# Six modulation chunks with buffers of their own, and a new order of the first loads, in a diffusion trunk step

## What is computed

```python
def ada_mods(cond, w, b):
    cond = cond.reshape(-1, D_MODEL)
    mod = (jax.nn.silu(cond) @ w + b)[:, None, :]
    return jnp.split(mod, 6, axis=-1)
...
    for i in range(DEPTH):
        sh1, sc1, g1, sh2, sc2, g2 = ada_mods(cond, ada_w[i], ada_b[i])
        h = modulate(rmsnorm(x, norm_mix[i]), sh1, sc1)
        ...
        x = x + g1 * mix
        h = modulate(rmsnorm(x, norm_ffn[i]), sh2, sc2)
        x = x + g2 * conv_ffn(h, ffn_w_in[i], ffn_conv_w[i], ffn_conv_b[i], ffn_w_out[i])
```

## Time and profile before

| | us |
|---|---|
| median of 3 runs | 2990.75 |
| lowest, highest | 2989.33, 2991.61 |
| profiled execution, first to last instruction (span) | 2988.2 |
| PE busy (share) | 2801.6 (94%) |
| DVE busy | 1607.8 (54%) |
| ACT busy | 1184.5 (40%) |
| POOL busy | 109.7 (4%) |

### The profile page before, as it was taken

How to read it: one execution, slowest core, us unless ns; L and a number is a source line. 1 busy time by engine, 2 the same in 40 slices (tenths; PEclk the granted TensorE clock), 3 DMA queues, 4 the chain that set the end, 5 groups by cost and what they waited for, 6 DMA issues and landing times.

```text
span 2988.2 us, 51513 instructions
## 1 busy us (share of the span) xinstructions
PE 2801.6 (94%) x19936; PEld 2645.5 (89%) x19936; DVE 1607.8 (54%) x2878; ACT 1184.5 (40%) x2042; POOL 109.7 (4%) x71
## 2 busy tenths in 40 slices
PE   5977799999998999999989999999998779999999
PEld 4965699999998999999969999999997569999999
DVE  2667556625644664366342665366367754663662
ACT  2347445414423552243232543244234754541441
POOL 1000010000002000000201000000100001000000
PEclk7989899999999999999989999999998989999999
DMA  6410133323320332333201332333121002221222
GB/s 233 181 64 1 50 125 134 137 74 135 136 93 33 138 134 103 123 133 130 66 24 57 120 134 100 111 134 127 63 78 36 1 15 61 78 84 64 73 85 74
DMA packets 62431, 279.67 MB, mean 94 GB/s; under 512 B 7392, under 2 KB 9568, under 8 KB 49632
## 3 DMA queue, kind: packets, MB, share of 16 engines
q1 hardware_dynamic: 62304, 277.93, 27.0%
HBM read 274.74 MB, written 3.16 MB: 93 GB/s over the span
## 4 chain that ended last, share of the span: by engine, by line
PE 86%; DVE 6%; ACT 6%; issue 2%; DMA 1%; SPq 0%; POOL 0%; DVEq 0%; ACTq 0%
PE ps L457 73%; ACT prob L923 3%; PE ps L541 3%; PE ps L480 3%; PE ps L743 1%; PE ps L552 1%; DVE prob L1265 1%; DVE prob L1282 1%; PE ps L502 1%; DMA ada_w<-in_ada_w 1%; ACT stat L925 1%; PE ps L680 1%; PE ps L649 1%; PE ps L510 1%; PE ps L635 1%
## 5 line engine op out<-in xcount | busy, mean ns | idle before, releaser
L457 PE MATMUL ps<-h_hi,w_hi 128*128 128x322 f32 x3392 | 799.8, 317 | 7.2 <-DVE w_lo L1057 4.1
L457 PE MATMUL ps<-h_lo,w_hi 128*128 128x322 f32 x3392 | 784.8, 313 | 0.0
L457 PE MATMUL ps<-h_hi,w_lo 128*128 128x322 f32 x3392 | 780.6, 312 | 0.0
L803 ACT ACTIVATE w_hi<-w_raw 128x1024 fp32r<-128x1024 f32 (+1 forms) x288 | 325.5, 1130 | 1037.1 <-PE ps L457 921.1
L457 PEld LDWEIGHTS ps<-h_hi,w_hi 128*128 128x128 f32 x3392 | 569.6, 190 | 34.0 <-issue 28.4
L457 PEld LDWEIGHTS ps<-h_lo,w_hi 128*128 128x128 f32 x3392 | 577.4, 190 | 0.0
L457 PEld LDWEIGHTS ps<-h_hi,w_lo 128*128 128x128 f32 x3392 | 577.0, 190 | 0.0
L1057 DVE TENSOR_TENSOR w_lo<-w_raw,w_hi 128x1024 fp32r<-128x1024 f32 (+1 forms) x288 | 377.3, 1310 | 67.6 <-ACT w_hi L803 65.9
L1177 DVE SCALAR_TENSOR_TENSOR x<-ps,mods,x 128x321 f32<-128x321 f32 (+5 forms) x264 | 99.9, 435 | 537.1 <-PE ps L457 537.1
L457 PE MATMUL ps<-f_hi,w_hi 128*128 128x322 f32 x1408 | 325.1, 312 | 0.0
L457 PE MATMUL ps<-f_hi,w_lo 128*128 128x322 f32 x1408 | 324.5, 312 | 0.0
(11 more groups left out here) (119 smaller groups left out, 2533.1 us busy)
## 6 DMA issues: line engine op xcount, KB each, us to landing
ada_w<-in_ada_w SPq DMA_DIRECT2D x96, 1024.0 KB, 5.5
w_raw<-in_w_in SPq DMA_DIRECT2D x176, 512.0 KB, 3.6
w_raw<-in_w_out SPq DMA_DIRECT2D x64, 704.0 KB, 4.0
w_raw<-in_w_qkv SPq DMA_DIRECT2D x24, 512.0 KB, 5.1
w_raw<-in_w_o SPq DMA_DIRECT2D x16, 512.0 KB, 3.8
w_raw<-in_w_fnet SPq DMA_DIRECT2D x8, 512.0 KB, 3.6
x<-in_x SPq DMA_DIRECT2D x1, 2576.0 KB, 15.5
out_y<-x SPq DMA_DIRECT2D x8, 322.0 KB, 3.7
```

Of the source, the lines that this page charges most:

```text
L457: mm = pe.matmul(ps[:, 2 * par + hf, 0:NH], w[par][:, kk, :], b[:, hf * NH:(hf + 1) * NH], start=(kk == 0 and n == 0), stop=(kk == k - 1 a ...
L803: act.activation(w_hi[par][:, 0:k, :], w_raw[par][:, 0:k, :], ACT.Copy).then_inc(hi_made, 1)
```

## The change

Chunks 2 to 7 get buffers of their own, `first_w`, that lie over the idle space of the ffn and the mixers, and semaphores of their own, so none of their loads waits. SP gives out nine constants, then chunks 0 and 1, `x`, chunks 2 to 7, the weights of units 0 and 1, and `conv` last. `conv` has its own semaphore, on which ACT and DVE wait ahead of the ffn of layer 0. Because the attention's tables go where `first_w` is, SP waits until all eight chunks are multiplied before it loads them. `chunk_turn` gives the count of earlier loads into an `ada_w` buffer, which is three less from chunk 8 on. What ACT, DVE, POOL and PE do, and in which order, is otherwise the same.

```diff
@@ buffers and semaphores
             tab_raw = sb("tab_raw", [P, 10, 512], F32, a)
+        with ExitStack() as a:
+            first_w = [sb(f"first_w{c}", [P, KT, AW], F32, a) for c in range(2, FIRST_CHUNKS)]
         stage_store = sb("stage_store", [P, 64 * 256 + 64])
...
+        first_in = [sem(f"first_in{c}") for c in range(2, FIRST_CHUNKS)]
+        conv_in = sem("conv_in")
...
-                  (pick, "pick"), (two_heads, "two_heads"), (ident, "ident"), (conv, "conv"),
+                  (pick, "pick"), (two_heads, "two_heads"), (ident, "ident"),
@@ SP
             for dst, src in CONSTS:
                 sp.dma_start(dst[:], t[src]).then_inc(const_in, 16)
-            load_units(0, 2)
             for c in range(2):
                 load_chunk(c, c, chunk_rows(c))
             sp.dma_start(x[:], t["x"]).then_inc(x_in, 16)
             for c in range(2, FIRST_CHUNKS):
-                load_chunk(c, c % 2, chunk_rows(c))
+                sp.dma_start(first_w[c - 2][:], chunk_rows(c)).then_inc(first_in[c - 2], 16)
+            load_units(0, 2)
+            sp.dma_start(conv[:], t["conv"]).then_inc(conv_in, 16)
+            sp.wait_ge(ada_mm, FIRST_CHUNKS)
@@ PE
+            def chunk_turn(c):
+
+                return c // 2 if c < 2 else c // 2 - (FIRST_CHUNKS - 2) // 2
+
             def ada_multiply(c, par, turn):
 
-                pe.wait_ge(ada_in[par], turn * 16 + 16)
+                if isinstance(c, int) and 2 <= c < FIRST_CHUNKS:
+                    weights = first_w[c - 2]
+                    pe.wait_ge(first_in[c - 2], 16)
+                else:
+                    weights = ada_w[par]
+                    pe.wait_ge(ada_in[par], turn * 16 + 16)
...
-                                       ada_w[par][:, 4 * r + j, :], start=(r == 0), stop=(r == 1),
+                                       weights[:, 4 * r + j, :], start=(r == 0), stop=(r == 1),
...
             for c in range(FIRST_CHUNKS):
-                ada_multiply(c, c % 2, c // 2)
+                ada_multiply(c, c % 2, chunk_turn(c))
@@ ACT, ahead of the ffn
+                if layer == 0:
+                    act.wait_ge(conv_in, 16)
@@ DVE, ahead of the ffn
+                if layer == 0:
+                    dve.wait_ge(conv_in, 16)
```

More of the change, by code:

```diff
@@ L664, in _ @@
                         if layer == 0 and FIRST_CHUNKS + n < NCH:
-                            ada_multiply(FIRST_CHUNKS + n, n % 2, (FIRST_CHUNKS + n) // 2)
+                            ada_multiply(FIRST_CHUNKS + n, n % 2, chunk_turn(FIRST_CHUNKS + n))
                         if layer == 0 and 12 < n <= NCH - FIRST_CHUNKS:
@@ L768, in _ @@
                     if not last:
-                        ada_multiply(c0, 0, c0 // 2)
+                        ada_multiply(c0, 0, chunk_turn(c0))
                     with pe.Fori(0, HALF // 2) as i:
@@ L778, in _ @@
                                 else:
-                                    ada_multiply(i * 2 + (c + 1), (c + 1) % 2, i + (c + 1) // 2)
+                                    ada_multiply(i * 2 + (c + 1), (c + 1) % 2, i + chunk_turn(c + 1))
                     if not last:
                         ada_turn(c0 + HALF - 1)
-                        ada_multiply(c0 + HALF, (c0 + HALF) % 2, (c0 + HALF) // 2)
+                        ada_multiply(c0 + HALF, (c0 + HALF) % 2, chunk_turn(c0 + HALF))
                     def gated(kk):
```

## The result

The changed kernel takes 3006.08 us (median of 4 runs, 3005.53 to 3007.95) against 2990.04 for the kernel before on the same chip (4 runs, 2988.77 to 2991.61). The ratio is 1.0057, 95% interval 1.0042 to 1.0071: 16.0 us slower. The forecast was 3006.4, the range 2999 to 3010.

What follows compares the result with a forecast made beforehand. PE carries 86% of the span, but the start hangs on the chain of waits up to copy 7. Copy 7 moving from 48.10 to 63.8 adds 15.7: 2990.75 + 15.7 = 3006.4 us, range 2999 to 3010.

Steps and rivals of the forecast that it cites:

- Where the loss is made: Start of the kernel: weights land at 36.5, w_lo ends at 38.8, copy 0 at 38.85, copy 7 at 63.8.
- The sum: First chunks' chain: copy 7 moves from 48.10 to 63.8, 15.7 us later, added to the median of 2990.75.
- The order on DVE as the cause: VectorE's queue is strictly first in, first out, so chunk copies wait behind late w_lo; otherwise 2 to 3 us gained.
- The gain it seemed to offer: Start: removed load waits bring copy 7 from 48.10 to 46.2, 1.9 us, plus about 0.8 for conv.
- that is 1.9 us: Chunk 7's 7.00 us load wait, less work left exposed: copy 7 at 46.2 instead of 48.10.
- The forecast of conv's worth: Constant loads: conv's 352 KB moved behind is worth about 0.8 us; its issue ahead of the large loads, 0.47.
- Covered work: ACT's squares, POOL's sums, SP's later tables and chunks, and conv waits stay hidden: 0 to 0.5 us together.
- Rival A, the clock: PE's clock rises in the copy chain: periods of 2.72 us, only +8.5 us, 2999.2; chance 12%.
- the one early period of 2.72 us: Rival A's support: one early gap between chunk copies on DVE, 19.18 - 16.46, against the usual 3.56 us.
- a granted clock of 0.50: Sign of being right: copies 0 to 7 at a 3.56 us pitch with the profile showing the 1.2 GHz level.
- Rival B, shared transfers: Loads issued together share the DMA engines, so weights land early: copy 7 at 45.3, 2.8 us gained, 2987.9; chance 4%.
- Rival C, slower transfers: Eleven queued large loads fall below 420 KB/us or hold SP: weights at 38.2, +17.4, 3008.2; within main upper range.

Runs made afterwards that it cites:

- Experiment 8: Changed kernel with PE's idle time in the first chunks' chain filled with unused matmuls, 4 behind each turn and 20 behind the last: 3003.89 us.
- experiments 3 to 5: Changed kernel with both w_lo behind eight copies (2992.26 us); also ACT squaring x before w_hi (2987.31); with that ACT order, w_lo behind copy 6 (2985.47).
- experiment 1: Changed kernel with only the two weight tiles loaded ahead of the chunks again: 2987.88 us against 2989.85, ratio 0.9993.

## Why the prediction was right

**Where the loss is made.** Right, step by step. The weights were forecast at 36.5 from the rate of the earlier trace rows; `w_hi` of unit 1 starts at 36.23. In between the DMA engines run at 425 GB/s and a share of 1.01, as before. That the end of the queue would be late as chunk 7 was (38.2) did not happen. `w_lo` ends at 38.55 (38.8 forecast), copy 0 stands at 38.47 (38.85; it overlaps the end of `w_lo`), copy 7 at 63.35 (63.8), the first product at 67.91 (68.4). The sum was 15.7, the first product is 15.24 later than in the trace that it was taken from.

**The order on DVE as the cause.** Shown by three runs: weights first, weights in the middle, and the order on DVE changed with the weights still last. What the Trainium skill says of VectorE's queue (TensorE: Matmul & The Clock Gate, Architectural detail), strictly first in, first out, and no row of before could show, was borne out: a copy whose input was ready at 12 us ran at 38.47.

**The gain it seemed to offer.** Here the step on chunk 7, "that is 1.9 us", was built on chance: its wait of 7.00 us was not in a second trace of the same kernel. The main sum did not use it, because the loop's 3.56 us set the pace. But the sum was made against a start that was 2.57 us slow, and its nearness to the measured 16.0 is in part luck: against the second trace copy 7 lies 17.8 us later and the span is 18.8 us longer, though that run, 2986.86, lies 2.7 us under the median of the others of its kernel. How the late start and the lucky later layers of the first trace are spread over all runs of the kernel before stays open. The forecast of conv's worth, 0.8 us and an issue of 0.47, fits the 1.2 measured.

**Covered work.** Right: the tables and the next chunks, issued from 62.35 on, held nobody, the squares of x ended at 47.8, and neither conv wait shows.

**Rival A, the clock.** It did not come: seven periods, all at 3.56 us, each multiply at 1.94. Experiment 8 shows that its mechanism is real, since the chain does run at 2.54 us once PE is kept busy, and the first product then runs at the high level at once, as rival A says. Its argument for, the one early period of 2.72 us, was a short stretch at the high level in that one trace (the turn there takes 0.61 us, not 1.02); in the second trace of the same kernel that period takes 3.56 us. One sign that I had given was wrong: "a granted clock of 0.50" in the new chain. The view by stretch (columns as in the earlier trace rows) says 1.00 there:

```profile
39.00:63.30 24.30, 20.16 (x140) 11.28 (x140) 2.96 (x12) 3.88 (x6) 10.46 (x7) 1.00 0.00 1
67.91:71.20 3.29, 3.29 (x12) 3.29 (x13) 3.29 (x8) 3.29 (x9) 0.00 (x0) 1.00 1.00 404
```

But a multiply of 1.94 us is that of the low level (1.07 at the high one), and products of 0.74 us are too. It seems that the record says 1.00 until its first change, in the trace of before up to 21 us as well. The level has to be read from durations there.

**Rival B, shared transfers.** Fell: loads landed in the order of issue, in experiments 3 to 5 chunk 2 by 21.4 us and unit 0's weights at 35.0, as the sum of the bytes ahead of them would have it. **Rival C, slower transfers:** SP was indeed held, 3.92 us at conv's issue, but the transfers did not slow down, so it cost nothing.

## What to carry to other kernels

Before a load is moved back, look for what is written behind its first consumer, on that consumer's engine: an engine in written order turns a late operand into a wait for everything behind it, also for work whose inputs are there. Move the consumer with the load, or leave both. Buffers of their own pay only if the loop that drains them waits for loads: at a period of 3.56 us the six were worth nothing here, at 2.54 us the traces give them 0.6 us, and more is not shown.

## What was not expected of the hardware

- VectorE's subtraction of two SBUF tensors took 2.52 us instead of 1.22 while GpSimd added SBUF tensors, and an operation of 0.17 us took 1.50. Copies out of PSUM (0.42 us) were not slower beside the same additions.
- How long the first products run at the low clock differs from kernel to kernel, 2.8 to 6.0 us, and between two executions of the kernel before, 2.8 and 3.8 us; a sooner start gave part of its gain back this way: products at the low level take 0.54 us a pair, from start to start, against 0.30.
- In the kernel with two buffers and fillings the clock had been high, PE then stood for 2.66 us, and the multiply behind this ran mostly at the low level (1.74 us). With the same fillings and six buffers PE stood nowhere longer than 0.76 us behind them, and every multiply from chunk 2 on took 1.07 us.
- SP's issue of loads, 0.43 to 0.5 us each, grew to 3.92 us for `conv` behind eleven large ones, with no loss of transfer rate. Their number alone isn't the reason: in experiment 1 the same eleven stand ahead of `conv` in another order, and its issue took 0.45 us. What is, stays open.
